# Routing stage of a one-core MoE layer: top four by match-and-replace, router on four column groups, norm in halves, half of a gather between up steps

## The reference, cut to what matters

```python
for l in range(DEPTH):                       # DEPTH = 1
    xn = rms_norm(h, norm_mix_g[l])          # h: 16 meta tokens + 256 tokens, 1024 wide
    ...                                      # latent attention and RG-LRU, gated and merged
    h = h + merged @ w_out[l]
    h = h + moe_ffn(rms_norm(h, norm_ffn_g[l]), ...)
h = rms_norm(h, norm_final_g)

def moe_ffn(...):
    logits = xt @ w_router + b_router        # 32 experts
    top_val, top_idx = lax.top_k(logits, 4)
    gates = softmax(top_val)
    # every token to its four experts; per expert:
    hdn = xb @ w_up[e] + b_up[e]             # 1024 -> 2048
    x_glu = jnp.minimum(hdn[:, :F], 7.0)
    x_lin = jnp.clip(hdn[:, F:], -7.0, 7.0)
    act = x_glu * jax.nn.sigmoid(1.702 * x_glu) * (x_lin + 1.0)
    y = act @ w_down[e] + b_down[e]          # 1024 -> 1024
    # weighted by the gate and added to its token
```

## Time and profile before

| | us |
|---|---|
| median of three runs | 1183.54 (1183.06 to 1183.62) |
| the profiled execution | 1183.1 |
| its span, first to last instruction | 1181.2 |
| PE busy in the span | 1146.4 (97%) |
| DVE busy | 228.2 (19%) |
| ACT busy | 188.3 (16%) |
| DMA moved | 442.03 MB, mean 374 GB/s |

### The profile page before, as it was taken

How to read it: one execution, slowest core, us unless ns; L and a number is a source line. 1 busy time by engine, 2 the same in 40 slices (tenths; PEclk the granted TensorE clock), 3 DMA queues, 4 the chain that set the end, 5 groups by cost and what they waited for, 6 DMA issues and landing times.

```text
span 1181.2 us, 13320 instructions
## 1 busy us (share of the span) xinstructions
PE 1146.4 (97%) x5598; PEld 532.9 (45%) x5598; DVE 228.2 (19%) x527; ACT 188.3 (16%) x406; POOL 0.2 (0%) x4
## 2 busy tenths in 40 slices
PE   9999999999999999999999999999999999998996
PEld 7767888855343333333343433333333333333332
DVE  4555620114111111111111111111111111111112
ACT  2257620002011110101010111101010101010102
POOL 0000000000000000000000000000000000000000
PEclk9999999999999999999999999999999999999999
DMA  9834434487999999999999999999999999999996
GB/s 378 341 148 179 150 110 166 151 336 295 396 414 436 432 427 432 432 431 432 433 432 431 433 433 428 435 433 427 434 435 427 434 434 428 434 434 427 428 426 261
DMA packets 26128, 442.03 MB, mean 374 GB/s; under 512 B 4144, under 2 KB 4656, under 8 KB 7408
## 3 DMA queue, kind: packets, MB, share of 16 engines
q1 hardware_dynamic: 23472, 439.19, 88.1%
q10 hardware_dynamic: 2624, 2.39, 0.6%
HBM read 440.52 MB, written 1.05 MB: 374 GB/s over the span
## 4 chain that ended last, share of the span: by engine, by line
PE 73%; DMA 25%; ACT 1%; DVE 0%; issue 0%; ACTq 0%; SPq 0%; another core or an unknown queue 0%; DVEq 0%
PE ps L881 28%; DMA ring<-in_w_exp_dram 17%; PE ps L900 12%; PE ps L539 11%; DMA work<-in_w_exp_dram 8%; PE ps L868 4%; PE ps L856 3%; PE ps L748 2%; PE ps L811 2%; PE ps L831 2%; PE ps L772 1%; PE ps L616 1%; ACT work L1298 1%; PE ps L890 1%; PE ps L582 1%; PE ps L862 1%
## 5 line engine op out<-in xcount | busy, mean ns | idle before, releaser
L881 PE MATMUL ps<-ring,work 128*64 128x512 f32 x1536 | 347.7, 604 | 10.9 <-DMA ring<-in_w_exp_dram 10.9
L881 PEld LDWEIGHTS ps<-ring,work 128*64 128x64 f32 x1536 | 111.1, 139 | 231.4 <-issue 223.9
L1736 DVE TENSOR_SCALAR work<-ps 128x512 f32<-128x512 f32 x32 | 22.1, 691 | 741.9 <-PE ps L881 741.9
L539 PE MATMUL ps<-work,ring 128*128 128x256 f32 (+2 forms) x576 | 129.6, 384 | 0.0
L900 PE MATMUL ps<-ring,work 128*64 128x512 f32 x512 | 113.6, 595 | 5.5 <-ACT work L1298 3.8
L900 PE MATMUL ps<-work 128*64 128x512 f32 x512 | 113.8, 595 | 4.2 <-ACT work L1298 3.8
L881 PE MATMUL ps<-work 128*64 128x512 f32 x512 | 116.0, 595 | 1.0 <-DMA work<-in_w_exp_dram 1.0
L539 PEld LDWEIGHTS ps<-work,ring 128*128 128x128 f32 (+1 forms) x576 | 107.1, 188 | 19.1 <-issue 1.2
L881 PEld LDWEIGHTS ps<-work 128*64 128x64 f32 x512 | 35.2, 137 | 76.8 <-issue 73.5
L900 PEld LDWEIGHTS ps<-ring,work 128*64 128x64 f32 x512 | 35.5, 137 | 73.4 <-issue 65.4
L900 PEld LDWEIGHTS ps<-work 128*64 128x64 f32 x512 | 35.2, 137 | 72.8 <-issue 62.8
(11 more groups left out here) (232 smaller groups left out, 618.0 us busy)
## 6 DMA issues: line engine op xcount, KB each, us to landing
ring<-in_w_exp_dram SPq DMA_DIRECT2D x52, 4096.0 KB, 40.6
work<-in_w_exp_dram SPq DMA_DIRECT2D x26, 4096.0 KB, 40.6
ring<-in_w_exp_dram SPq DMA_DIRECT2D x23, 2048.0 KB, 9.9
ring<-in_w_mix_dram SPq DMA_DIRECT2D x29, 1024.0 KB, 7.3
work<-in_w_exp_dram SPq DMA_DIRECT2D x10, 2048.0 KB, 12.1
work<-in_w_exp_dram SPq DMA_DIRECT2D x4, 1024.0 KB, 43.2
ring<-in_w_exp_dram SPq DMA_DIRECT2D x2, 1024.0 KB, 5.7
ring<-in_w_mix_dram SPq DMA_DIRECT2D x2, 576.0 KB, 17.8
```

What stands on the lines that cost most here:

```text
L539: ins = nc.tensor.matmul(ps[part:part + width, b, 0:hi - lo], wv[:, k, o:o + width], xnT[:, k, lo:hi], start=(k == 0), stop=(k == KT - 1))
L881: ins = nc.tensor.matmul(ps[CAP * c:CAP * c + CAP, b, :], xeT[:, k, CAP * (u % 2):CAP * (u % 2) + CAP], wu[:, k % SPAN, 512 * q:512 * q + ...
L1736: V.tensor_scalar(hg, ps[:, 0, :], LIMIT, None, ALU.min).then_inc(glu_ready, 1)
```

## The change

Four edits, all between the output projection and the end of expert 0's up product.

- **Top four.** The logits stand behind four columns of +3.0e38 (`lgs`, 36 columns), so that the eight largest are these four and the four largest logits. `match_replace` writes a copy in which those eight are replaced, and the mask is where copy and logits differ. It is done tile by tile (`choose`), and `mask_ready` counts two. The exponentials' bias is the fifth of the eight.
- **Router.** `wr` is the stationary operand (32 columns), the transposed tokens the moving one (128), in four column groups; block k and block k+4 share a group. ScalarE copies the 128x128 result (`logT`), and a matmul with `pick_e` (`fold`) adds the four groups and turns them back.
- **Norm in halves.** Tile 1's squares are summed in two halves; the second half's sum goes into the root with the first as its bias. `xn2` of tile 1 is written in halves too (`xn2_ready` counts three), and `fetch(1, 4)` waits for the third. `turn_h` is called by halves.
- **Order.** `gather(1)` is issued behind up step 1, `seed(0, 1)` behind step 2, `seed(1, 0)` behind step 3, `router(1)` behind `seed(0, 0)`. `pick` is made from the ranks directly (the slot numbers now begin at 1), ahead of the position table. ScalarE issues its two bias DMAs ahead of the second gather copy. `selm` now lies in the room of the second selector, which therefore waits for the position matmuls.

```diff
-            spe.wait_ge(xn2_ready, TT)
+            spe.wait_ge(xn2_ready, TT + 1)
             fetch(1, 4)
...
+            def turn_h(i, c):
+                pe.wait_ge(h_half, 2 * i + c + 1)
+                for k in range(4 * c, 4 * c + 4):
+                    ins = nc.tensor.transpose(ps[:, 4 + 2 * i + c, P * (k % 4):P * (k % 4) + P],
                                               X[:, i, P * k:P * k + P], ident)
-                    if k % 4 == 3:
-                        ins.then_inc(hT_done, 1)
+                ins.then_inc(hT_done, 1)
...
-                    ins = nc.tensor.matmul(ps[:, i, 0:E], hT[:, k, :], wr[:, k, :], start=(k == 0), stop=(k == KT - 1))
-                ins.then_inc(logits_done, 1)
+                    q = E * (k % 4)
+                    ins = nc.tensor.matmul(ps[q:q + E, 0, 0:P], wr[:, k, :], hT[:, k, :], start=(k < 4), stop=(k >= 4))
+                ins.then_inc(logT_done, 1)
+            def fold(i):
+                pe.wait_ge(logT_ready, i + 1)
+                nc.tensor.matmul(ps[:, 1, E * i:E * i + E], logT, pick_e[:, 0:E], start=True, stop=True).then_inc(logits_done, 1)
...
                         if r == 2:
-                            turn_h(0)
+                            turn_h(0, 0)
+                            turn_h(0, 1)
                 if i == 0:
                     ins.then_inc(out_done, 1)
             pe.wait_ge(wr_ready, 1)
             router(0)
-            turn_h(1)
-            router(1)
+            turn_h(1, 0)
+            fold(0)
+            turn_h(1, 1)
...
             seed(0, 0)
+            router(1)
+            fold(1)
             pe.wait_ge(sel0_ready, 1)
             pe.wait_ge(logits_read, 1)
             up_bias(0)
-            seed(0, 1)
...
+            pe.wait_ge(mask_ready, 2)
             nc.tensor.matmul(ps[:, 2, E:2 * E], upper, selm[:, 1, :], start=False, stop=True, skip_group_check=True)\
...
-            seed(1, 0)
             pe.wait_ge(xn2_ready, TT)
             pe.wait_ge(pick_ready, 2)
             pe.wait_ge(counts_read, 1)
             gather(0).then_inc(gather_done, 1)
-            gather(1).then_inc(gather_done, 1)
             seed(1, 1).then_inc(seeded, 1)
...
             def first_between(k):
+                if k == 1:
+                    pe.wait_ge(xn2_ready, TT + 1)
+                    gather(1).then_inc(gather_done, 1)
+                if k == 2:
+                    seed(0, 1)
+                if k == 3:
+                    seed(1, 0)
                 if k == 4:
...
+            def read_logT(i):
+                act.wait_ge(logT_done, i + 1)
+                nc.scalar.activation(logT, ps[:, 0, 0:P], ACT.Copy).then_inc(logT_ready, 1)
+            act.wait_ge(h_half, 2)
+            nc.scalar.activation(sqx[:, 0, :], X[:, 0, :], ACT.Square, accum_out=ss2[:, 0:1]).then_inc(h_sumsq, 1)
+            read_hT(0)
+            act.wait_ge(h_var, 1)
+            nc.scalar.activation(rs2[:, 0:1], ss2[:, 0:1], ACT.Sqrt).then_inc(h_std, 1)
+            read_logT(0)
+            act.wait_ge(h_half, 3)
+            nc.scalar.activation(sqx[:, 1, 0:512], X[:, 1, 0:512], ACT.Square, accum_out=ss2[:, 1:2]).then_inc(h_sumsq, 1)
+            read_hT(1)
+            act.wait_ge(h_half, 4)
+            nc.scalar.activation(sqx[:, 1, 512:1024], X[:, 1, 512:1024], ACT.Square, accum_out=ss2h).then_inc(h_sumsq, 1)
+            act.wait_ge(h_sumsq, 3)
+            act.wait_ge(h_var, 2)
+            nc.scalar.activation(rs2[:, 1:2], ss2h, ACT.Sqrt, bias=ssb, scale=1.0 / D).then_inc(h_std, 1)
+            read_logT(1)
...
-            for h in range(2):
-                act.wait_ge(gather_done, h + 1)
-                read_gather(h)
+            act.wait_ge(gather_done, 1)
+            read_gather(0)
             act.wait_ge(seeded, 1)
-            act.wait_ge(xn2_ready, TT)
+            act.wait_ge(xn2_ready, TT + 1)
             act.wait_ge(hT_done, 2 * TT)
             for c in range(2):
                 act.dma_start(y[CAP * c:CAP * c + E, :], b_down[0, :, 512 * c:512 * c + 512]).then_inc(bdn_in, 16)
+            act.wait_ge(gather_done, 2)
+            read_gather(1)
...
-                return V.max(t8[:, i, :], lg[:, i, :])
-            def normed(i):
-                V.scalar_tensor_tensor(out=xn2[:, i, :], in0=X[:, i, :], scalar=rs2[:, i:i + 1], in1=gffn,
+                link(V.max(t8[:, i, :], lgs[:, i, :]))
+            def choose(i):
+                link(V.match_replace(topless[:, i, :], t8[:, i, :], lgs[:, i, :], MASKED))
+                V.tensor_tensor(selm[:, i, :], topless[:, i, TOP_K:], lg[:, i, :], ALU.not_equal).then_inc(mask_ready, 1)
+            def normed(i, lo, hi):
+                V.scalar_tensor_tensor(out=xn2[:, i, lo:hi], in0=X[:, i, lo:hi], scalar=rs2[:, i:i + 1], in1=gffn[:, lo:hi],
...
+                    V.memset(lgs[:, :, 0:TOP_K], -MASKED)
+                    dve.wait_ge(h_sumsq, 1)
+                    V.tensor_scalar(ss2[:, 0:1], ss2[:, 0:1], 1.0 / D, EPS, ALU.mult, ALU.add).then_inc(h_var, 1)
+                else:
+                    dve.wait_ge(h_sumsq, 2)
+                    V.tensor_scalar(ssb, ss2[:, 1:2], 1.0 / D, EPS, ALU.mult, ALU.add).then_inc(h_var, 1)
+                    logits(0)
...
                 if i == 1:
...
+                    choose(0)
                 dve.wait_ge(h_std, i + 1)
                 link(V.reciprocal(rs2[:, i:i + 1], rs2[:, i:i + 1]))
-                if i == 0:
-                    normed(0)
...
-            ins = logits(1)
-            link(ins)
-            V.tensor_scalar(nm1.rearrange("p (i k) -> p i k", k=1), t8[:, :, 0:1], -1.0, None, ALU.mult)
...
-            V.tensor_tensor(eq, lg, k4, ALU.is_equal)
-            link(V.tensor_tensor(gt, lg, k4, ALU.is_gt))
-            link(V.tensor_reduce(ngt, gt, AX_X, ALU.add))
...
-            link(V.scalar_tensor_tensor(out=eq, in0=rank, scalar=TOP_K + 0.5, in1=eq, op0=ALU.is_lt, op1=ALU.mult))
-            V.tensor_tensor(selm, gt, eq, ALU.add).then_inc(mask_ready, 1)
-            normed(1)
...
+                normed(i, 0, D if i == 0 else 512)
+            logits(1)
+            V.tensor_scalar(nm1.rearrange("p (i k) -> p i k", k=1), t8[:, :, TOP_K:TOP_K + 1], -1.0, None, ALU.mult)
+            choose(1)
+            normed(1, 512, D)
+            dve.wait_ge(mask_ready, TT)
             dve.wait_ge(pos_done, 1)
             link(V.scalar_tensor_tensor(out=rank, in0=ps[:, 2, 0:TT * E].rearrange("p (i e) -> p i e", i=TT), scalar=1.0,
                                         in1=selm, op0=ALU.add, op1=ALU.mult))
+            V.tensor_tensor(pick, slot_id.rearrange("p (i u t) -> p i u t", i=1, u=2).broadcast_to([P, TT, 2, CAP]),
+                            rank[:, :, 0:2].rearrange("p i (u t) -> p i u t", t=1).broadcast_to([P, TT, 2, CAP]),
+                            ALU.is_equal).then_inc(pick_ready, 2)
             for j in range(BLOCKS + 1):
                 w = min(E, NCOL - E * j)
...
-                ins = V.scalar_tensor_tensor(out=posm[:, :, E * j:E * j + w], in0=rank[:, :, 0:w], scalar=-1.0,
-                                             in1=bb, op0=ALU.add, op1=ALU.subtract)
-                if j == 0:
-                    link(ins)
-                    pick_tokens(0).then_inc(pick_ready, 2)
+                ins = V.scalar_tensor_tensor(out=posm[:, :, E * j:E * j + w], in0=rank[:, :, 0:w], scalar=1.0,
+                                             in1=bb, op0=ALU.mult, op1=ALU.subtract)
+            link(ins)
...
             route(0)
+            dve.wait_ge(pos_done, 2)
             select(1, 1).then_inc(route_ready, 1)
```

More of the change, by code:

```diff
@@ L111, in constants @@
     b[:, slice(*CB["upper"])] = np.triu(np.ones((P, P), np.float32), 1)
-    b[:, slice(*CB["slot_id"])] = np.arange(P) % CAP
+    b[:, slice(*CB["slot_id"])] = np.arange(P) % CAP + 1
     n = np.arange(NCOL)
@@ L238, in layer @@
         sel = view(2 * CAP, LATE + 4608).rearrange("p (b t) -> p b t", b=2)
+        selm = view(TT * E, LATE + 4608 + CAP).rearrange("p (i e) -> p i e", i=TT)
         xeT = view(KT * P, LATE + 4736).rearrange("p (k t) -> p k t", k=KT)
@@ L243, in layer @@
         wr = view(KT * E, LATE + 5760).rearrange("p (k e) -> p k e", k=KT)
-        tmp = view(6 * E, LATE + 5760).rearrange("p (k e) -> p k e", k=6)
-        selm = view(TT * E, LATE + 5952).rearrange("p (i e) -> p i e", i=TT)
+        rank = view(TT * E, LATE + 5760).rearrange("p (i e) -> p i e", i=TT)
         pick = view(TT * P, LATE + 6016).rearrange("p (i u t) -> p i u t", i=TT, u=2)
         upper = view(P, LATE + 6016)
+        logT = view(P, LATE + 6144)
         gpick = view(TT * P, LATE + 6272).rearrange("p (i t) -> p i t", i=TT)
-        lg = view(TT * E, LATE + 6272).rearrange("p (i e) -> p i e", i=TT)
-        brt = view(E, LATE + 6336)
-        block_base = view(NCOL, LATE + 6368)
+        lgs = view(TT * (TOP_K + E), LATE + 6272).rearrange("p (i e) -> p i e", i=TT)
+        lg = lgs[:, :, TOP_K:]
+        brt = view(E, LATE + 6344)
```

(43 more changed lines are left out.)

9 lines of the change are left out of this document (removed).

## The result

The changed kernel takes 1184.06 us (median of 20 runs, 1183.19 to 1186.93). The kernel before, measured beside it, takes 1183.12 us (20 runs, 1182.37 to 1183.73). The ratio is 1.0012, with a 95% interval of 1.0006 to 1.0017: slower by 0.94 us between the medians and 1.4 by the ratio, inside the 0.2% that the prediction called "same". The forecast was 1183.7, 0.2 us over the 1183.54 from which it was counted; the shift came out at 0.9. What the median hides is the spread: these 20 runs of before lie within 1.4 us, the changed kernel's within 3.7.

The account below looks back on a forecast made before the run. The weight stream, full from about 309 us, bounds the kernel through the issue at 306.75. Up starting 4.04 us sooner against 4.25 us of insertions gives +0.2 us: median 1183.7 us from 1183.54, range 1182.0 to 1185.8.

Parts of the forecast that it names:

- What bounds the kernel: Weight stream full from about 309 us; the end moves with the issue at 306.75; 4.3 us of empty queue recoverable at most.
- The router: Routing stage on PE: each router takes 0.65 us in four column groups, saving 1.2 to 1.3 us of work.
- Rival B: Routers' column groups don't run beside each other: tile 1's router takes 1.97 us, +1.3 us, total 1185.0; chance 0.05.
- Match-and-replace: Top four on DVE: taken as 0.4 us, bounds 0.2 to 0.85, with second mask at 274.05, 1.7 us sooner.
- Rival D: Top four: a long match-and-replace, some 3 us, would make the end 2.4 us later (1186.1); chance 0.03.
- Start of up: Expert 0's up product starts at 278.66 against 282.70, 4.04 us sooner.
- Insertions in up: Second gather half and two seeds behind up steps 1 to 3 cost 4.25 us together, bounds 3.6 to 4.7.
- The deciding issue: SP's transfer needing the first half of expert 0's down product goes at 306.95 instead of 306.75.
- Rival C: PE's clock falls to 1.2 GHz before 306 us; one stretch costs 1.9 us, two 3.8; chances 0.03 and 0.03.
- the comparison of gaps: Routing-stage PE gaps of 0.3 to 0.6 us look like those at 298 to 304 us, where 2.4 GHz held.
- A granted clock of 0.5 before 330 us: Sign of a wrong prediction: PE's granted clock at 0.5 anywhere before 330 us.
- The size of it all: DVE chain 2.25 us shorter, but seeds that filled PE's waits now cost 2.2 in the open; end of up +0.2 us.

Follow-up runs that it names:

- e2: Changed kernel with the stream's first two pieces for expert 2 held until the third up step; fastest 1183.59 us, median 1185.30 us.
- e1: The changed kernel run again with nothing edited, for its spread and a second trace; fastest 1183.55 us, median 1184.78 us.
- e8: Changed kernel with both seeds moved out of up into PE's waits, second gather half still behind up step 1; fastest 1181.33 us, median 1181.91 us.
- e7: Changed kernel with the first seed also moved into up, behind step 5, leaving PE one more gap; fastest 1186.01 us, median 1187.12 us.
- e5: Changed kernel with both seeds put into PE's waits and the second gather half ahead of up; median 1181.37 us, ratio to before 0.9985.
- e4: Changed kernel with five 128-column dummy matmuls, thrown away, in PE's three gaps of the routing stage; fastest 1183.34 us, median 1183.66 us.

## Why the prediction was right, and where it was off

*What bounds the kernel.* Right, and the strongest part: the stream is full from 309 us on, the end hangs on one issue, and the issues before it don't count (e2, and the constant rest in ten traces). The idle time in front of the deciding issue is as said, 1.9 us forecast and 2.0 measured; the 1.8 us in front of the unit for step 4 were not foreseen.

*The router.* 0.65 us forecast from the sum of squares at L565, 0.65 measured. Rival B did not occur. The rule of the Trainium skill ("TensorE: Matmul & The Clock Gate", Part 3) that weight loads overlap only where row groups differ does not hold here either, since 16 loads of 0.11 us each take 0.38 us, beside the 0.65 us of the router's matmuls.

*Match-and-replace.* 0.4 us taken, 0.26 measured, covered either way. The second mask was there 5.49 us after the start of the residual add (273.45 - 267.96) against 5.64 forecast (274.05 - 268.41). Rival D did not occur.

*Start of up.* Forecast 10.25 us after the residual add began, measured 10.40, so 3.89 us sooner than before instead of 4.04. Of the 0.15 us, 0.10 lies in the three position matmuls (0.85 us for 0.75) and the rest ahead of them; the rank and the pick took what was forecast.

*Insertions in up.* This is the term that was mis-sized: 4.25 us forecast, within bounds of 3.6 to 4.7, and 4.56 measured. The row it rests on, 3.58 against 3.43 us for 16 instructions, gives a switch of 0.15 back into up, and that is right for each of the three (1.87 for 8 instead of 1.72). A seed takes 1.06 us of its own, not the 0.96 that it takes behind a gather, and the gather half 1.98 (281.95 to 283.93) instead of 1.90. The stage came out at +0.67 us instead of +0.2. Two of the prediction's own sums are loose: its terms give 4.27 and, with no switches, 3.5 rather than 3.6; and the bounds with 0.5 for the chain reach from 1182.5 to 1184.7 us, not to 1185.2. The median lies within either.

*The deciding issue.* Forecast at 306.95, seen at 306.97, but this is flattered: the mixer ended 0.45 us sooner, and that hid most of the 0.47 by which the stage was underestimated.

*The clock.* Rival C had a chance of 0.06, and by the tail it happens in about half of the executions (9 of 20 runs of after and 6 of 11 of e1 are over 1184.6 us). Its price was set at 1.9 us for one stretch; the one in e2 cost 1.44, the longer one in e7 2.7. The step that failed is the comparison of gaps. I took the stretch of 298 to 304 us, where PE had gaps and stayed at 2.4 GHz, for a likeness of the new one. That stretch, expert 0's activation with waits of 1.02, 0.46 and 0.26 us, keeps its clock in all ten traces, and in after it looks as it did in before:

```profile
298.00:304.00 6.00, 4.26 (x26) 1.45 (x24) 3.35 (x7) 1.56 (x4) 0.00 (x0) 1.00 1.01 393
```

PE is idle there for 1.7 of 6 us, in the routing stage for 1.6 of 8, yet it is in the routing stage that the clock fell in two of the ten. So the idle share was no measure of likeness. What it is about the routing stage's gaps, their number, their place or the work between them, no run here separates. The median is 0.9 us over before's because of 0.67 us of stage and this tail; the profiled run, being free of it, shows only the former. A granted clock of 0.5 before 330 us was named as a sign of being wrong; it does not show in the trace of after, and does in those of e2 and e7.

*The size of it all.* The reason that so large a rearrangement moved the time by some 0.1% was right: without the seeds in up the stage is 1.20 us shorter than before's (e8), and the seeds, which used to stand in waits, take 1.86 us of it back.

## What to carry to other kernels

Where a transfer queue is full from some point on, look for the last issue before it fills and measure each edit by how it moves that one. Work that stood in an engine's waits cost nothing here, and moved behind them it was paid in full, with its switches: shorten the chain by what you like, but leave fillers in the waits (e5 against after: 2.2 us of the stage). And a TensorE with several short gaps in a stretch can lose as much to its clock as to the gaps or more (e2: 1.4 us beside gaps of 1.6), in some executions only, so take the spread of the runs as a reading of its own.

## What the runs showed of the hardware

- Gaps of only 0.4 to 0.5 us were followed by a fall of the granted clock to 1.2 GHz in some executions (e2 and e7; not in the traces of after and e1). The 16 instructions of a gather half then took 3.46 to 3.75 us instead of 2.02. With five dummy matmuls in the gaps (e4) none of 11 runs lay in the tail.
- Four column groups with different stationary operands run side by side: 8 float32 matmuls of 128x32 by 128x128, 16 instructions, in 0.65 us, against 1.87 for 8 of 128x128 by 128x32, and 2.02 for the 16 instructions of 128x128 by 128x128 in the gather half.
- A match-and-replace of 8 values in 36 columns is two VectorE instructions, 0.08 and 0.18 us.
- The first tile's stage began at 267.81 to 268.80 us of the span in ten traces of kernels with the same mixer. What makes the mixer end up to 1 us apart wasn't tried.
